# The down weights of experts 4 to 63: requested from ScalarE's queue, behind the first half of the output copy

## The chip, the core and the metric

The kernel runs on one core of a Trainium2 chip. The metric is the time of one execution on the device in microseconds (us); the median of several runs counts. The core has five engines that run side by side and wait for each other by semaphores: TensorE (PE in the profile, its weight loads PEld), VectorE (DVE), ScalarE (ACT), GpSimd (POOL) and SyncE (SP). Sixteen DMA engines move data between the device memory and the on-chip memory. They take their work from queues, which SyncE, ScalarE or GpSimd fill.

## The reference, cut to what matters

One layer of a decoder: a mixer of two recurrent branches, a normalisation, then a mixture of experts with a shared expert, a gated embedding, and a second normalisation. The change lies in the 64 routed experts:

```python
for c in range(N_EXPERTS // EXPERT_CHUNK):          # 64 experts in all
    g = jnp.einsum('td,edf->tef', xt, w_gate[sl])
    u = jnp.einsum('td,edf->tef', xt, w_up[sl])
    hdn = jax.nn.silu(g) * u * combine[:, sl, None]
    y = y + jnp.einsum('tef,efd->td', hdn, w_down[sl])
```

There are 512 tokens of 1,024 values, each sent to 8 of 64 experts. An expert has gate and up weights of 1,024 x 256 and down weights of 256 x 1,024, in 32-bit floats, 1 MB each. Tokens are gathered by expert in tiles of 96 rows.

## The kernel before

The expert stage runs from about 760 to 1,416 us of the profiled execution. Every expert takes the same steps, one expert after the other:

- GpSimd gathers the expert's rows from device memory, four experts ahead (the gather, line 663).
- SyncE requests the weights: `load_in` gate and up (two DMAs of 1 MB, line 522), `load_down` the down weights (one DMA of 1 MB, line 525). There are four buffers of each kind, so the weights of expert e + 4 go where those of expert e were. Gate and up may be requested once TensorE has done the gate and up products of expert e (semaphore `g_e_put`), the down weights once it has done the down products of expert e (`y_e_put`).
- Products are made in three passes of a faster number format: ScalarE makes the high part of the weights (`gate_up_high`, `down_high`), VectorE subtracts it to get the low part (`gate_up_low`, `down_low`), and TensorE multiplies high by high, low by high and high by low (lines 732 to 734). Line 1169 is the helper for all ScalarE operations, line 1425 that for VectorE's element-wise ones.
- TensorE works in the order: gate and up products of expert u, turning of the rows of expert u + 1 (8 transposes, line 739), down products of expert u - 1, turning of the hidden values of expert u (2 transposes).
- `y_kept` copies the result out of two banks of TensorE's memory, the first half on ScalarE (96 x 512), the second on VectorE (line 1984). GpSimd then adds the rows into `acc_dram` in device memory (`add_rows`, line 677, the scatter below). One scatter is issued only when the one before has landed, and `y_kept` of an expert waits until the scatter of two experts before has landed (`rows_added`), since there are two buffers `yb`.

The order on every engine is written out by hand. ScalarE's, in `expert`: high part of the next gate and up weights, silu, high part of the next rows, high part of this expert's down weights, `y_kept` of the expert before, high part of the hidden values. SyncE's is a loop over the experts: wait for `g_e_put`, request gate and up, wait for `y_e_put`, request down. Since TensorE makes the down products of expert u - 1 only after the gate and up products of expert u, SyncE stands at `y_e_put` of expert u - 1 when `g_e_put` of expert u is already there, and gate and up of expert u + 4 are requested behind it.

Of the kernel before, what the change touches and what calls it, by code (L numbers as in the profile page):

```python
# [42 lines left out]
E = 64  # L43
# [30 lines left out]
def decoder_layer(nc, A, out):  # L74
# [9 lines left out]
    with ctx:  # L84
# [14 lines left out]
        def sem(name):  # L99
            return ctx.enter_context(nc.semaphore(name))  # L100
# [164 lines left out]
        dn_row = [v.rearrange("p k c -> p (k c)") for v in dn]  # L265
# [79 lines left out]
        S = {n: sem(n) for n in names}  # L345
# [3 lines left out]
        s_wdn = [sem(f"expert_down{u}") for u in range(4)]  # L349
# [6 lines left out]
        def wait(eng, s, v):  # L356
            if not isinstance(v, int) or v > 0:
                eng.wait_ge(s, v)
# [17 lines left out]
        for h in range(CB // HD):  # L376
            r0 = h * HD
            while r0 < (h + 1) * HD:
                n = min((h + 1) * HD, (r0 // P + 1) * P) - r0
                PIECES.append((h, r0 - h * HD, n, r0 // P, r0 % P))  # L380
                r0 += n
        PAIRS = [(k, m) for m in range(ML) for k in range(ML)
                 if any(t == k and h * HD < (m + 1) * P and (h + 1) * HD > m * P for h, _, _, t, _ in PIECES)]
        LRU_BANKS = [2, 3, 0, 1, 2, 3]
        G_BANKS = [3, 0, 1]

        @block.sync
        def _(sp):
# [129 lines left out]
            w_down_e = A["moe_w_down"][0].rearrange("e (p k) c -> e p (k c)", k=2)  # L518

            def load_in(e, u, done):  # L520
                for w, src in enumerate((w_gate_e, w_up_e)):
                    sp.dma_start(gu_row[u][w], src[bass.ds(e, 1)].rearrange("o p x -> p (o x)")).then_inc(done, 16)

            def load_down(e, u, done):
                sp.dma_start(dn_row[u], w_down_e[bass.ds(e, 1)].rearrange("o p x -> p (o x)")).then_inc(done, 16)
# [21 lines left out]
            with sp.Fori(0, E // 4 - 1) as i:  # L547
                for u in range(4):
                    sp.wait_ge(S["g_e_put"], 4 * i + (u + 1))
                    load_in(4 * i + (4 + u), u, s_wgu[u])  # L550
                    sp.wait_ge(S["y_e_put"], 4 * i + (u + 1))
                    load_down(4 * i + (4 + u), u, s_wdn[u])

            sp.wait_ge(S["y_e_put"], E)
            sp.wait_ge(S["texp_ready"], 1)
# [1 line left out]
            with sp.If(n_over > 0):  # L557
                with sp.Fori(0, OV) as i:
                    with sp.If(i < n_over):
                        e = sp.value_load(texpi[0:1, bass.ds(i, 1)].bitcast(i32), min_val=0, max_val=E - 1)  # L560
# [606 lines left out]
        def _(act):  # L1167
            def f(out_, in_, func, **kw):
                return nc.scalar.activation(out_, in_, func, **kw)  # L1169
# [167 lines left out]
            def rows_high(i, u):  # L1337
                act.wait_ge(S["xT_e_put"], 4 * i + u + 1)
                for h in range(2):
                    f(xe_hi[:, 4 * h:4 * h + 4], banks[h][:, 0:4 * SL].rearrange("p (k x) -> p k x", k=4),  # L1340
                      ACT.Copy).then_inc(S["xT_e_high"], 1)

            def gate_up_high(i, u):
                act.wait_ge(s_wgu[u % 4], 32 * i + 32 * (u // 4 + 1))
                wait(act, S["g_e_put"], 4 * i + u - 1)
                for k in range(2):
                    for w in range(2):
                        ks = slice(KD * w + 4 * k, KD * w + 4 * k + 4)
                        f(gu_hi[u % 2][:, w, 4 * k:4 * k + 4], gu_raw[u % 4][:, ks], ACT.Copy).then_inc(S["gu_e_high"], 1)


            def down_high(i, u):
                act.wait_ge(s_wdn[u % 4], 16 * i + 16 * (u // 4 + 1))
                wait(act, S["y_e_put"], 4 * i + u - 1)
                if isinstance(i, int) and i == 0 and u == 1:
                    act.wait_ge(S["acc_stored"], 16 * TT)
                f(dn_hi[u % 2], dn[u % 4][:, 0], ACT.Copy).then_inc(S["dn_e_high"], 1)

            def hid_high(i, u):
                act.wait_ge(S["hT_e_put"], 4 * i + u + 1)  # L1360
                f(heT_hi[u % 2], banks[4][:, 0:SL], ACT.Copy).then_inc(S["hT_e_high"], 1)

            def y_kept(i, u):
                wait(act, S["rows_added"], 64 * i + 16 * (u - 1))
                act.wait_ge(S["y_e_put"], 4 * i + u + 1)
                f(yb[u % 2][:, 0:512], banks[5][0:SL, :], ACT.Copy).then_inc(S["y_e_act"], 1)

            def expert(i, u, more=True):
                if more:
                    gate_up_high(i, u + 1)  # L1370
                act.wait_ge(S["g_e_put"], 4 * i + u + 1)
                wait(act, S["hT_e_put"], 4 * i + u - 1)
                f(hid_e[u % 2], banks[2 + u % 2][0:SL, 0:F], ACT.Silu).then_inc(S["silu_e"], 1)
                if more:
                    rows_high(i, u + 1)
                down_high(i, u)
                if not isinstance(i, int) or u >= 1:
                    y_kept(i, u - 1)
                hid_high(i, u)

            def sh_silu(t):
# [12 lines left out]
            for u in range(0, 5):  # L1394
                expert(0, u)
            with act.Fori(1, E // 4 - 1) as i:
                for u in range(1, 5):
                    expert(i, u)
            for n in range(E - 3, E):
                expert(0, n, more=n + 1 < E)  # L1400
            y_kept(0, E - 1)

            act.wait_ge(S["texp_ready"], 1)
# [667 lines left out]
```

## Time and profile before

| | us |
|---|---|
| median of 3 runs | 1435.78 (1435.25 to 1435.85) |
| the profiled execution, whole | 1443.62 |
| its span, first to last instruction | 1441.9 |
| expert stage, first expert's rows high to the last scatter landed | about 779 to 1416 |
| TensorE busy in the span | 1371.3 (95%) |
| ScalarE busy | 689.6 (48%) |
| VectorE busy | 978.7 (68%) |

Times inside the execution are counted from the start of the span. The busy share of TensorE is counted from matmuls that overlap, so it doesn't say that TensorE is never late; the time between the same operation of two neighbouring experts (the period) says more. A DMA's landing is the time from its issue to the moment its semaphore is full. The profile gives it for the down weights and the scatters; for gate and up, which share one semaphore, the chain of work shows it.

### The profile page before, as it was taken

How to read it: one execution, taken by the hardware profiler on the slowest of the kernel's cores; microseconds unless marked ns; L12 is line 12 of the kernel's file. 1: busy time of each engine (PE TensorE's matmuls, PEld its weight loads, DVE VectorE, ACT ScalarE, POOL GpSimd, SP SyncE). 2: the span in 40 equal slices, each digit the busy share in tenths (PEclk: the TensorE clock that was granted, in tenths of full speed). 3: DMA queues.
4: the chain of work that ended last, by engine and by line, in shares of the span. 5: the costliest groups of instructions: out<-in, count | busy, mean ns of one | idle time of the engine just before them, and what ended most of it. 6: DMA issues, size and time to landing. Idle time of an engine off the chain costs nothing.

```text
span 1441.9 us, 19598 instructions
## 1 busy us (share of the span) xinstructions
PE 1371.3 (95%) x6615; PEld 983.6 (68%) x6615; DVE 978.7 (68%) x1419; ACT 689.6 (48%) x990; POOL 485.3 (34%) x380
## 2 busy tenths in 40 slices
PE   7979999999999999999999999999999999999990
PEld 6766777777788888885545666666666666666660
DVE  7997868786611211558626888888778788788775
ACT  4233654638422222210023776766766667667650
POOL 0231534435444444000010333334344443343422
PEclk8998999999999999999999999999999999999996
DMA  8044253534233333741057999999999999999964
GB/s 257 3 132 72 76 74 81 86 66 106 80 95 95 95 102 106 307 164 67 0 200 305 347 368 363 359 363 371 366 372 365 370 375 367 372 368 362 371 201 131
DMA packets 140775, 315.82 MB, mean 219 GB/s; under 512 B 18112, under 2 KB 99696, under 8 KB 115312
## 3 DMA queue, kind: packets, MB, share of 16 engines
q1 hardware_dynamic: 126384, 281.50, 55.8%
q0 software_dynamic: 14336, 33.59, 9.7%
q8 instruction: 35, 0.57, 0.2%
q14 instruction: 20, 0.16, 0.0%
HBM read 297.27 MB, written 34.54 MB: 230 GB/s over the span
## 4 chain that ended last, share of the span: by engine, by line
PE 67%; DVE 12%; DMA 9%; DVEq 4%; issue 3%; POOL 2%; ACT 2%; POOLq 1%; SPq 1%; ACTq 0%
PE bank L732 16%; PE bank L734 15%; PE bank L733 15%; DMA gate_up<-moe_w_up_in 8%; DVE arena L1425 6%; PE bank L1104 6%; DVEq L1422 4%; PE bank L739 4%; PE bank L891 3%; PE bank L969 2%; PE bank L989 1%; DVE arena L1713 1%; POOLq L632 1%; DVE arena L1428 1%; POOL arena L633 1%
## 5 line engine op out<-in xcount | busy, mean ns | idle before, releaser
L1425 DVE TENSOR_TENSOR gate_up_low<-gate_up,gate_up_high 128x1024 fp32r<-128x1024 f32 x256 | 296.4, 1219 | 89.4 <-ACT gate_up_high L1169 89.4
L1169 ACT ACTIVATE gate_up_high<-gate_up 128x1024 fp32r<-128x1024 f32 x256 | 249.6, 1048 | 85.5 <-DMA gate_up<-moe_w_up_in 85.5
L1169 ACT ACTIVATE arena<-bank 96x512 f32<-96x512 f32 (+5 forms) x244 | 129.1, 553 | 255.8 <-PE bank L734 132.1
L677 POOL DMA_INDIRECT acc_dram<-arena x64 | 118.5, 1851 | 333.7 <-DMA acc_dram<-arena 291.6
L1425 DVE TENSOR_TENSOR arena<-arena 128x512 f32<-128x512 f32 (+12 forms) x296 | 206.7, 730 | 16.6 <-ACT arena L1169 3.6
L732 PE MATMUL bank<-gate_up_high,rows_high 128*96 128x512 f32 x512 | 206.9, 404 | 4.1 <-DVE rows_low L1425 3.7
L734 PE MATMUL bank<-gate_up_high,rows_low 128*96 128x512 f32 x512 | 203.0, 396 | 0.0
L733 PE MATMUL bank<-gate_up_low,rows_high 128*96 128x512 f32 x512 | 201.6, 394 | 0.0
L739 PEld LDWEIGHTS bank<-arena 96*128 96x128 f32 (+5 forms) x1001 | 127.3, 186 | 53.2 <-issue 37.4
L595 POOL TENSOR_TENSOR wb_low<-arena,wb_high 128x1024 fp32r<-128x1024 f32 (+1 forms) x40 | 107.1, 2682 | 147.7 <-ACT wb_high L1169 147.7
L739 PE MATMUL bank<-arena 96*128 96x96 f32 (+5 forms) x1001 | 127.3, 266 | 7.6 <-DMA arena<-x_in 4.5
L595 POOL TENSOR_TENSOR wa_low<-arena,wa_high 128x1024 fp32r<-128x1024 f32 x24 | 62.8, 2627 | 202.3 <-ACT wa_high L1169 202.3
L1104 PE MATMUL bank<-down,arena 128*96 128x512 f32 x256 | 130.6, 592 | 0.0
L660 POOL COPY arena<-arena 96x1 int32 (+1 forms) x64 | 70.5, 1101 | 128.3 <-DVEq L1422 81.7
L1169 ACT ACTIVATE wb_high<-arena 128x1024 fp32r<-128x1024 f32 (+1 forms) x40 | 45.6, 1145 | 138.4 <-DMA arena<-w_glu_in 74.2
L732 PEld LDWEIGHTS bank<-gate_up_high,rows_high 128*96 128x96 f32 x512 | 84.0, 164 | 38.8 <-DVE rows_low L1425 5.4
L734 PEld LDWEIGHTS bank<-gate_up_high,rows_low 128*96 128x96 f32 x512 | 82.9, 162 | 36.3
L1431 DVE SCALAR_TENSOR_TENSOR arena<-bank,arena 128x511 f32<-128x511 f32 (+3 forms) x44 | 32.2, 747 | 109.6 <-PE bank L734 105.0
L733 PEld LDWEIGHTS bank<-gate_up_low,rows_high 128*96 128x96 f32 x512 | 83.3, 163 | 32.3 <-issue 0.3
L1169 ACT ACTIVATE arena<-arena 128x512 f32<-128x512 f32 (+5 forms) x54 | 31.6, 609 | 154.1 <-DVE arena L1425 80.8
L663 POOL DMA_INDIRECT arena<-x_dram,arena x64 | 76.5, 1195 | 55.8 <-DVE arena L1984 31.3
L732 PE MATMUL bank<-x_high,wa_high 128*128 128x512 f32 x192 | 77.8, 405 | 8.9 <-DVE arena L1431 7.0
(172 smaller groups left out, 2645.8 us busy)
## 6 DMA issues: line engine op xcount, KB each, us to landing
gate_up<-moe_w_gate_in SPq DMA_DIRECT2D x64, 1024.0 KB
gate_up<-moe_w_up_in SPq DMA_DIRECT2D x64, 1024.0 KB
down<-moe_w_down_in SPq DMA_DIRECT2D x64, 1024.0 KB, 16.2
arena<-w_in_in SPq DMA_DIRECT2D x40, 512.0 KB, 4.0
arena<-w_glu_in SPq DMA_DIRECT2D x16, 512.0 KB, 3.9
arena<-w_lru_out_in SPq DMA_DIRECT2D x8, 768.0 KB, 4.8
arena<-x_in SPq DMA_DIRECT2D x8, 512.0 KB, 5.1
wu<-w_in_in SPq DMA_DIRECT2D x8, 512.0 KB, 6.2
```

The costliest lines, as they stand in the source:

```text
L595: nc.gpsimd.tensor_tensor(lo, w, hi.bitcast(f32), ALU.subtract).then_inc(S["w_split"], 1)
L660: nc.gpsimd.tensor_copy(idxcol[:, u:u + 1].bitcast(i32), idxT[:, bass.ds(e, 1)].bitcast(i32)).then_inc(S["slot_col"], 1)
L663: nc.gpsimd.indirect_dma_start(out=xg[u], out_offset=None, in_=x1_dram, in_offset=bass.IndirectOffsetOnAxis(ap=idxcol[:, u:u + 1].bitcast( ...
L677: nc.gpsimd.indirect_dma_start(out=acc_dram, out_offset=bass.IndirectOffsetOnAxis(ap=idxcol[:, 4 + c:5 + c].bitcast(u32), axis=0), in_=yb[ ...
L732: mm(dst, w_hi, v_hi, start=start, stop=False)
L733: mm(dst, w_hi, v_lo, start=False, stop=False)
L734: return mm(dst, w_lo, v_hi, start=False, stop=stop)
L739: return nc.tensor.transpose(dst, src, ident[0:n, 0:n])
L1104: last = mm(banks[5 + hf][0:SL, :], heT[u % 2], dn[u % 4][:, 1, hs], start=False, stop=True)
L1169: return nc.scalar.activation(out_, in_, func, **kw)
L1422: dve.drain()
L1425: return V_.tensor_tensor(out_, a, b_, op)
```

## The change

SyncE's loop no longer requests the down weights of experts 4 to 63; it only waits for `g_e_put` and requests gate and up. ScalarE requests them in `expert`, behind `y_kept` of the expert before, and ahead of the high part of the hidden values. The wait that protects the buffer is the one that `y_kept` makes anyway (`y_e_put`). The down weights of experts 0 to 3 stay with SyncE.

```diff
                 for u in range(4):
                     sp.wait_ge(S["g_e_put"], 4 * i + (u + 1))
                     load_in(4 * i + (4 + u), u, s_wgu[u])
-                    sp.wait_ge(S["y_e_put"], 4 * i + (u + 1))
-                    load_down(4 * i + (4 + u), u, s_wdn[u])
...
-            def expert(i, u, more=True):
+            w_down_e = A["moe_w_down"][0].rearrange("e (p k) c -> e p (k c)", k=2)
+
+            def expert(i, u, more=True, more_down=True):
...
                 if not isinstance(i, int) or u >= 1:
                     y_kept(i, u - 1)
+                    if more_down:
+                        nc.scalar.dma_start(dn_row[(u - 1) % 4], w_down_e[bass.ds(4 * i + (u + 3), 1)].rearrange("o p x -> p (o x)")
+                                            ).then_inc(s_wdn[(u - 1) % 4], 16)
                 hid_high(i, u)
...
             for n in range(E - 3, E):
-                expert(0, n, more=n + 1 < E)
+                expert(0, n, more=n + 1 < E, more_down=False)
```

SyncE's queue in the loop over the experts, before (two of the four experts of a turn; `gate_up_169` and `down_173` are the first pair of buffers, `gate_up_170` and `down_174` the second; the REGISTER_ALU and ISA rows work out addresses and counts):

```order
L522 ISA [waits g_e_put]
L522 DMA gate_up_169<-moe_w_gate_in 128x2048
L522 DMA gate_up_169<-moe_w_up_in 128x2048
L525 DMA down_173<-moe_w_down_in 128x2048 [waits y_e_put]
L549 REGISTER_ALU
L522 ISA [waits g_e_put]
L522 DMA gate_up_170<-moe_w_gate_in 128x2048
L522 DMA gate_up_170<-moe_w_up_in 128x2048
L525 DMA down_174<-moe_w_down_in 128x2048 [waits y_e_put]
```

And in the changed kernel:

```order
L522 ISA [waits g_e_put]
L522 DMA gate_up_169<-moe_w_gate_in 128x2048
L522 DMA gate_up_169<-moe_w_up_in 128x2048
L549 REGISTER_ALU
L522 ISA [waits g_e_put]
L522 DMA gate_up_170<-moe_w_gate_in 128x2048
L522 DMA gate_up_170<-moe_w_up_in 128x2048
```

The request of the down weights and its wait for `y_e_put` are gone from between two pairs of gate and up.

ScalarE's queue in the same loop, before, one expert (the ACTIVATE of 96x256 is the silu, that of 96x512 is `y_kept`):

```order
L1169 ACTIVATE arena<-bank 96x256 [waits hT_e_put,g_e_put]
L1338 REGISTER_ALU
L1169 ACTIVATE rows_high<-bank 128x384 [waits xT_e_put]
L1169 ACTIVATE rows_high<-bank 128x384
L1169 ACTIVATE down_high_189<-down_175 128x1024 [waits y_e_put,expert_down2]
L1169 ACTIVATE arena<-bank 96x512 [waits y_e_put,rows_added]
L1169 ACTIVATE hidden_high_185<-bank 128x96 [waits hT_e_put]
L1344 REGISTER_ALU
L1169 ACTIVATE gate_up_high_179<-gate_up_169 128x1024 [waits g_e_put,expert_in0]
```

And in the changed kernel (its helper for ScalarE stands at line 1167):

```order
L1167 ACTIVATE arena<-bank 96x256 [waits hT_e_put,g_e_put]
L1167 ACTIVATE rows_high<-bank 128x384 [waits xT_e_put]
L1167 ACTIVATE rows_high<-bank 128x384
L1167 ACTIVATE down_high_189<-down_175 128x1024 [waits y_e_put,expert_down2]
L1167 ACTIVATE arena<-bank 96x512 [waits y_e_put,rows_added]
L1380 ISA
L1380 DMA down_174<-moe_w_down_in 128x2048
L1167 ACTIVATE hidden_high_185<-bank 128x96 [waits hT_e_put]
L1342 REGISTER_ALU
L1167 ACTIVATE gate_up_high_179<-gate_up_169 128x1024 [waits g_e_put,expert_in0]
```

The request stands behind `y_kept` without a wait of its own, with one instruction for its address ahead of it, and `hidden_high` and the next `gate_up_high` stand behind it.

## Rows read from the trace of the kernel before

**Rows 1.** The page: DMA busy share and GB/s in 40 slices.

```profile
DMA  8044253534233333741057999999999999999964
GB/s 257 3 132 72 76 74 81 86 66 106 80 95 95 95 102 106 307 164 67 0 200 305 347 368 363 359 363 371 366 372 365 370 375 367 372 368 362 371 201 131
```

**Rows 2.** Busy time by stretch: PE, PEld, DVE, ACT, POOL, clock, DMA share, GB/s.

```profile
788.00:792.00 4.00, 4.00 (x21) 2.81 (x20) 1.84 (x4) 2.20 (x4) 0.00 (x0) 1.00 0.00 0
796.00:800.00 4.00, 4.00 (x23) 3.09 (x22) 3.65 (x4) 2.26 (x5) 3.11 (x4) 1.00 0.97 358
960.00:980.00 20.00, 20.00 (x91) 13.57 (x91) 16.66 (x22) 12.78 (x20) 7.83 (x8) 1.00 1.02 355
1100.00:1120.00 20.00, 19.76 (x90) 13.37 (x89) 16.03 (x22) 13.58 (x21) 8.64 (x8) 1.00 1.02 373
```

**Rows 3.** The DMA queues in the 100 us from 1060, ten experts.

```profile
q1 hardware_dynamic: 4361, 31.76, 81.1%
q0 software_dynamic: 2240, 5.19, 21.3%
```

**Rows 4.** The chain that ended last: start us, us, what.

```profile
779.00 0.87 PE bank L739 x8
...
1032.44 0.86 PE bank L739 x8
...
1336.01 22.26 DMA gate_up<-moe_w_up_in
...
1371.19 0.86 PE bank L739 x8
...
1380.93 0.86 PE bank L739 x8
...
1390.67 0.86 PE bank L739 x8
```

**Rows 5.** SyncE's queue in order of time: start us, us, request; the first experts.

```profile
792.91 0.33 SPq L525 DMA_DIRECT2D down<-moe_w_down_in  x1
793.51 0.76 SPq L522 DMA_DIRECT2D gate_up<-moe_w_gate_in  x1
...
802.65 0.33 SPq L525 DMA_DIRECT2D down<-moe_w_down_in  x1
```

**Rows 6.** ScalarE in order of time: silu of experts 1 and 2; idle in brackets.

```profile
788.95 0.38 ACT L1169 ACTIVATE arena<-bank 96x256 f32<-96x256 f32 x1 [3.32 <-PE bank L734]
...
798.69 0.38 ACT L1169 ACTIVATE arena<-bank 96x256 f32<-96x256 f32 x1 [1.26 <-PE bank L734]
```

**Rows 7.** ScalarE around the place of the new request, a late expert.

```profile
1106.73 0.59 ACT L1169 ACTIVATE arena<-bank 96x512 f32<-96x512 f32 x1 [0.89 <-PE bank L1104]
...
1109.71 3.90 ACT L1169 ACTIVATE gate_up_high<-gate_up 128x1024 fp32r<-128x1024 f32 x4 [2.25 <-DMA gate_up<-moe_w_up_in]
```

**Rows 8.** An early expert, VectorE's last row part and TensorE's product behind it.

```profile
858.50 1.02 DVE L1425 TENSOR_TENSOR rows_low<-bank,rows_high 128x384 fp32r<-128x384 f32 x2 [0.37 <-ACT rows_high L1169]
...
861.03 0.45 PE L732 MATMUL bank<-gate_up_high,rows_high 128*96 128x512 f32 x1
```

**Rows 9.** Landing of the down weights: 790 to 880 us, then 1,100 to 1,390 us.

```profile
DMA to landing us min/median/max: 7.1/7.8/8.6
...
DMA to landing us min/median/max: 15.2/16.2/17.0
```

**Rows 10.** Landing of the scatters: 1,100 to 1,388 us, then 1,388 to 1,442 us.

```profile
DMA to landing us min/median/max: 6.4/9.0/9.8
...
DMA to landing us min/median/max: 4.4/4.6/5.1
```

**Rows 11.** GpSimd, two scatters in a row; and the next output copy on ScalarE.

```profile
1104.90 2.13 POOL L677 DMA_INDIRECT acc_dram<-arena  x1 [4.92 <-DMA acc_dram<-arena]
...
1114.79 1.96 POOL L677 DMA_INDIRECT acc_dram<-arena  x1 [4.63 <-DMA acc_dram<-arena]
...
1116.95 0.59 ACT L1169 ACTIVATE arena<-bank 96x512 f32<-96x512 f32 x1 [1.35 <-PE bank L1104]
```

## Prediction

> **What bounds the kernel now.** I read the slices of the page first: from the 24th on the DMA row says 9 and about 365 GB/s without a break [rows 1]. The busy time by stretch sharpens this: the DMA engines stand at 1.02 both at 960 us, where TensorE has no gap, and at 1,100 us, where it is short of 20 us by 0.24 [rows 2]. So in the expert stage the DMA engines are full, and the question is how close behind them TensorE is.
>
> The chain answers that. The 8 transposes of line 739 come once per expert. The first time stands at 779.00, the last at 1390.67, and there are 62 periods between: 611.67 / 62 = 9.87 us. Where TensorE never waits, the period is 1380.93 - 1371.19 = 9.74 us. From 1032.44 to 1390.67 there are 36 periods, 358.23 us, and 36 x 9.74 is 350.6: the starving of TensorE costs 7.6 us in all. The chain gives its cause: it runs through landings of `up` weights in the late part, the last for 22.26 us from 1336.01 to 1358.3. Behind that landing the period is 9.74 again (1371.19, 1380.93, 1390.67) [rows 4]. So **the end of the kernel hangs on the moment at which that late pair of gate and up weights has landed**; it moves as this landing moves, and the most that can be won is 7.6 us.
>
> How much DMA work is an expert? In 100 us with ten experts the queue of the weights took 81.1% of the engines and that of gathers and scatters 21.3% [rows 3]: 8.1 us and 2.1 us per expert, together 102%, since packets overlap a little. A third of 8.1, **2.7 us, is the price of 1 MB of weights**.
>
> **Part 1: gate and up are requested earlier.** SyncE stands at `y_e_put` while `g_e_put` is there. For the sixth expert: the pair is requested at 793.51, behind the down request of 792.91 [rows 5], though the silu that waits for the same `g_e_put` starts at 788.95 [rows 6]. The change requests it about 0.1 us after, at 789.1, 4.4 us earlier. This holds for 59 experts, but in a full queue an earlier request only waits longer. It counts where the DMA engines are idle, and that is in one place: 788 to 792 us, share 0.00, and full again by 796 us [rows 2]. There the engines start 4.4 us earlier. They then have 3 loads (the pair, and the down weights, which come at 793.6), 8.1 us, and are through at about 797.3; the next pair may be requested at 798.8, behind the silu of 798.69 [rows 6], where today the work lasts until 793.5 + 8.1 = 801.6 and the next request comes at 802.65 with scatter and gather between. So a new hole of 1.5 us opens, and 4.4 - 1.5 = **2.9 us** of DMA time are won. Bounds: 1.9 (the loads run a tenth faster than in the crowd, and the hole is 2.5) and 4.4 (no hole, scatter and gather fill it).
>
> **Part 2: the down weights go through another queue.** In one queue, requests are served in their order: the down weights of expert e stand behind gate and up of e, and land 16.2 us after the request in the late part, 7.8 us in the early part [rows 9]. In the changed kernel the request is ScalarE's, its queue holds nothing else, and SyncE's queue is full. Take the pair requested today right behind the down request that follows the `y_kept` of 1106.73, at about 1107.6; with the 22.3 us of the chain's landing [rows 4] it lands at 1129.9. In the changed kernel its down weights are requested about one period after 1107.3, the end of `y_kept` [rows 7], at 1117.2, that is 12.7 us ahead of the landing of the pair. If two queues share the engines, a load of 2.7 us takes 5.4 us, and 2.1 us more for gather and scatter: it lands at about 1125, ahead of the pair that is needed first. So one more load is served before each late `up` weight: **+2.7 us** on the landing that sets the end. Bounds: 0 (the engines serve by time of request) and 4.0 (half of the following down load gets ahead as well).
>
> That the engines mix queues shows in the scatters: one lands after 9.0 us while the weights' queue is full and after 4.6 us when it is empty [rows 10]; it is slowed, but it doesn't wait for the 16 to 22 us of requests ahead of it. The Trainium skill ("DMA: Bandwidth & Descriptors", section "Queues, rings and completion order") says that each DMA engine takes packets in turn from the queues that have work. By that rule part 2 costs 2.7 us; by service in time order it would cost nothing, and no run so far shows two such queues of weights.
>
> **Part 3: the request itself on ScalarE.** A request took 0.33 us on SyncE, and from one to the next, with the address, 0.60 us (792.91 to 793.51) [rows 5]. The trace has none on ScalarE; I take 0.6 us, once per expert, with 0.3 and 1.2 (twice the value) as bounds. What is queued behind: `hidden_high`, and the next `gate_up_high`. In the late part `gate_up_high` first waits 2.25 us for the DMA [rows 7], which hides 0.6 and 1.2 alike. In the early part there is no such wait, and the cover is further down: VectorE's last part of the rows ends at 858.50 + 1.02 = 859.52 and TensorE starts the product at 861.03 [rows 8], 1.5 us later. So part 3 costs 0. If the cover were gone it would cost up to 0.6 us per expert. SyncE loses a request and a wait, which nobody waits for. The down weights of the last experts have over 10 us to spare in both orders.
>
> **The sum**, against the profiled execution: -2.9 + 2.7 + 0 = -0.2 us on a span of 1441.9 us; the execution of 1443.6 us stays at 1443.4. The runs that count lie at 1435.8, so 1435.6. Bounds: -4.4 + 0 = -4.4 and -1.9 + 4.0 = +2.1, thus **1431.4 to 1437.9** for this case.
>
> **Rival A: the scatters become the bound (slower).** They are a chain of their own: 1104.90, next 1114.79, that is 9.89 us, and GpSimd waits for the landing of the one before [rows 11]. The period of the experts is 9.95 us there. The landing at 1114.8 is 2.2 us ahead of the `y_kept` at 1116.95 that needs it. One full queue beside them lengthens a scatter from 4.6 to 9.0 us, by 4.4 us [rows 10]. ScalarE's queue is a second one, and has work for 5.4 of every 9.95 us, beginning right where a scatter is under way. If it slows the scatter in the same measure, that is 4.4 x 5.4 / 9.95 = 2.4 us; it decides from 0.1 us on, since the chain has no more room, and after 2.2 / 2.4, about one expert, `y_kept` waits on ScalarE with everything behind it. Against it: as soon as the period is longer than the 10.2 us that the DMA work of an expert takes by [rows 3], the engines have pauses and the crowding goes. So the period settles between 9.95 and 10.2. At 10.1 from the start: 62 x (10.1 - 9.87) = +14 us, **1450**; at 10.2 it is +20, and with 0.1 us of slowing it is +3. The early part speaks against it too: there the scatters keep up with a period of 9.74 us, so they have a little room. The rule of turns that the Trainium skill's page on DMA states makes this rival likelier, since a third queue with work takes a turn of its own; that can't be seen in the trace of before.
>
> **Rival B: the earlier requests count in full (faster).** If down weights don't get ahead, or two queues keep the engines a little fuller than one, the landings come 2.9 to 4.4 us earlier, and at most the 7.6 us of starving go: 1428.2 to 1432.9, taken as **1431**. For it: TensorE has nothing else to wait for. Against it: the share is 1.02 already.
>
> **Rival C: ScalarE's request is dear (slower).** If it held ScalarE for 3 us, more than the 2.25 and the 1.5 us of cover, 0.8 to 1.5 us per expert would show, 60 x 1 = +60 us. SyncE's 0.33 us speak against it. And that the change does nothing, because its requests come no earlier, is excluded by the 4.4 us between [rows 5] and [rows 6]; what is left of that case is the forecast.
>
> **How the numbers follow.** Forecast 0.45, rival A 0.34, B 0.17, C 0.04. About 0.2% (2.9 us) can be told from no change. The forecast's own range reaches below that bound a little: faster 0.17 + 0.04 = 0.21; of rival A a part (slowing of some tenths) stays below it: slower 0.31 + 0.04 = 0.35; same 0.44. The range that should hold 8 in 10 goes from 1430 to 1452: below it lies half of B, above it C and the dear end of A.
>
> **What would show it.** Part 1: in the stretch 788 to 792 us the DMA share is no longer 0, and the pair's request stands at 789. Part 2: the down weights land in about 8 us in the late part instead of 16; the landings of `up` take some 4 us longer counted from their request. Part 3: `gate_up_high` still waits for the DMA in the late part. Rival A: landings of scatters over 9.5 us, a `y_kept` on ScalarE that waits for `acc_dram`, and pauses in the DMA share. The forecast is wrong if the period in the late part leaves 9.95 by more than 0.1 us.

## The result, and the profile after

The changed kernel takes 1445.65 us, median of 4 runs (1443.33 to 1446.72), against 1435.82 for the kernel before beside it (1435.25 to 1439.39). The ratio is 1.0061, with a 95% interval of 1.0045 to 1.0077: it is slower, by 9.8 us. Timed again with the last experiments (e11_after_again) it gave 1445.5 us and 1.006 [1.0041, 1.0078].

The two profiled executions hide this. The changed kernel's took 1443.33 us with a span of 1441.6 us, that of before 1443.62 and 1441.9. The reason lies ahead of the change's place. VectorE's first and last output copy frame the expert stage; start, duration, engine and operation, before and then after:

```profile
792.92 0.69 DVE L1984 COPY arena<-bank 96x512 f32<-96x512 f32 x1
...
1408.49 0.69 DVE L1984 COPY arena<-bank 96x512 f32<-96x512 f32 x1 [3.63 <-PE bank L1104]
```

```profile
783.81 0.69 DVE L1987 COPY arena<-bank 96x512 f32<-96x512 f32 x1
...
1408.05 0.69 DVE L1987 COPY arena<-bank 96x512 f32<-96x512 f32 x1 [3.63 <-PE bank L1102]
```

The stage itself, from its first to its last output copy, went from 615.6 to 624.2 us, **+8.7 us**, while in the execution of before everything ahead of it took 9.1 us longer (in 100 to 200 us its granted clock was 0.95, and 1.00 in the other). From here on this stage time is what is compared. It comes from one execution of each kernel; the changed kernel's, taken twice, differs by 1.2 us (624.2 and 625.4).

The wait that grew is in the groups of the page. Of the changed kernel, two of ScalarE and one of GpSimd (busy, mean ns, then idle time and its releaser):

```profile
L1167 ACT ACTIVATE arena<-bank 96x512 f32<-96x512 f32 (+5 forms) x244 | 129.3, 553 | 337.6 <-DMA acc_dram<-arena 155.2
L1167 ACT ACTIVATE gate_up_high<-gate_up 128x1024 fp32r<-128x1024 f32 x256 | 249.4, 1049 | 2.7 <-issue 2.3
...
L675 POOL DMA_INDIRECT acc_dram<-arena x64 | 99.3, 1552 | 320.7 <-DMA acc_dram<-arena 286.7
```

ScalarE's output copies (96x512) now wait 155.2 us for the landing of scatters, and `gate_up_high` no longer waits for weights at all; in [rows 7] it was the other way round. The chain that ended last says the same: its share of DMA was 9%, mostly `up` weights [rows 4 show one of them], and now it is

```profile
PE 39%; DMA 36%; DVE 11%; issue 5%; DVEq 4%; POOL 2%; POOLq 2%; ACT 1%; SPq 0%; ACTq 0%
```

nearly all of the 36% landings of scatters into `acc_dram`. Here is the same place as in [rows 7], a late expert on ScalarE, in order of time:

```profile
1107.32 0.60 ACT L1167 ACTIVATE arena<-bank 96x512 f32<-96x512 f32 x1 [2.74 <-DMA acc_dram<-arena]
1107.47 0.34 ACTq L1380 DMA_DIRECT2D down<-moe_w_down_in  x1
1107.86 0.25 ACT L1167 ACTIVATE hidden_high<-bank 128x96 fp32r<-128x96 f32 x1
1108.01 3.89 ACT L1167 ACTIVATE gate_up_high<-gate_up 128x1024 fp32r<-128x1024 f32 x4
```

The copy waited 2.74 us for a scatter; the request took 0.34 us of ScalarE's queue; what stands behind it waits for nothing.

**Where in the stage the time went.** In blocks of ten experts, from one output copy on ScalarE to the tenth after it:

| experts | 1-10 | 11-20 | 21-30 | 31-40 | 41-50 | 51-60 |
|---|---|---|---|---|---|---|
| before | 97.4 | 97.4 | 99.0 | 100.0 | 98.1 | 100.2 |
| changed | 97.4 | **106.1** | 99.3 | 100.9 | 98.7 | 98.4 |

The whole loss is in one block; the four blocks behind it sum to 397.3 us in both kernels. What happens in the long block is seen in ScalarE's output copies, 9.73 us apart up to 890.98 and then 10.7, 11.6 and 11.0:

```profile
881.25 0.59 ACT L1167 ACTIVATE arena<-bank 96x512 f32<-96x512 f32 x1 [1.35 <-PE bank L1102]
890.98 0.59 ACT L1167 ACTIVATE arena<-bank 96x512 f32<-96x512 f32 x1 [1.35 <-PE bank L1102]
901.70 0.59 ACT L1167 ACTIVATE arena<-bank 96x512 f32<-96x512 f32 x1 [2.33 <-DMA acc_dram<-arena]
913.26 0.59 ACT L1167 ACTIVATE arena<-bank 96x512 f32<-96x512 f32 x1 [4.16 <-DMA acc_dram<-arena]
924.27 0.59 ACT L1167 ACTIVATE arena<-bank 96x512 f32<-96x512 f32 x1 [4.45 <-DMA acc_dram<-arena]
```

and in the chain of work of the same stretch (start, us, what), which holds nothing but scatters and GpSimd's 0.9 us between them:

```profile
868.23 10.02 DMA acc_dram<-arena
...
879.15 10.82 DMA acc_dram<-arena
...
890.87 10.80 DMA acc_dram<-arena
...
902.58 10.66 DMA acc_dram<-arena
...
947.47 9.29 DMA acc_dram<-arena
```

10.8 + 0.9 is 11.7 us per scatter in this stretch; from the second expert to the twelfth it is 10.7 on average, while an expert takes 9.73. So the scatter falls behind its output copy, from 1.9 us at the second expert to 11.6 us at the twelfth. There the two buffers `yb` are used up, and the output copy, hence TensorE, goes at the pace of the scatters.

The DMA share has no pauses in this (busy time by stretch, columns as in [rows 2]):

```profile
920.00:960.00 40.00, 36.97 (x159) 24.16 (x159) 29.25 (x42) 22.95 (x35) 15.78 (x15) 1.00 1.02 367
1100.00:1120.00 20.00, 18.82 (x84) 12.42 (x83) 17.99 (x24) 14.82 (x23) 10.38 (x11) 1.00 1.02 351
```

TensorE is busy for 37 of 40 us at 920 to 960, and the DMA engines for all of them. So they moved weights that nobody waited for yet. That lead comes back nowhere: the changed kernel's engines run dry earlier at the end. Before, and then after:

```profile
1370.00:1380.00 10.00, 10.00 (x47) 6.82 (x46) 8.31 (x12) 7.02 (x11) 2.50 (x2) 1.00 1.02 361
1380.00:1400.00 20.00, 20.00 (x91) 13.57 (x90) 14.85 (x21) 10.92 (x18) 6.04 (x6) 1.00 0.58 178
```

```profile
1370.00:1380.00 10.00, 10.00 (x47) 6.82 (x46) 8.83 (x13) 7.50 (x11) 3.63 (x4) 1.00 0.79 261
1380.00:1400.00 20.00, 20.00 (x92) 13.59 (x91) 13.92 (x20) 9.71 (x18) 6.64 (x6) 1.00 0.36 51
```

With the stage ending at 1408 in both, before has 10 x 1.02 + 20 x 0.58 = 21.8 us of DMA work left from 1370 on, after has 10 x 0.79 + 20 x 0.36 = 15.1: the changed kernel has fetched weights worth 6.7 us sooner than needed. That this lead was piled up in the long block alone isn't shown: the smaller hole at the start of the stage (below, part 1) also gave the engines a few us.

### The profile page after: what moved, and what is told of

It is laid out like the page before. It is cut to its first block, busy times and chain, and to the rows that moved or that the text cites. A ratio compares the mean times of both kernels' runs of the same rounds, so it can differ in the third digit from the quotient of the medians.

```text
span 1441.6 us, 19610 instructions
## 1 busy us (share of the span) xinstructions
PE 1370.1 (95%) x6615; PEld 979.8 (68%) x6615; DVE 978.7 (68%) x1419; ACT 690.4 (48%) x990; POOL 505.6 (35%) x380
## 4 chain that ended last, share of the span: by engine, by line
PE 39%; DMA 36%; DVE 11%; issue 5%; DVEq 4%; POOL 2%; POOLq 2%; ACT 1%; SPq 0%; ACTq 0%
DMA acc_dram<-arena 35%; PE bank L730 9%; PE bank L732 9%; PE bank L731 8%; DVE arena L1428 6%; DVEq L1425 4%; PE bank L889 3%; PE bank L967 2%; PE bank L987 1%; DVE arena L1716 1%; POOLq L630 1%; POOL arena L631 1%; PE bank L1061 1%; DVE arena L1431 1%; PE bank L737 1%
## 5 line engine op out<-in xcount | busy, mean ns | idle before, releaser
L1167 ACT ACTIVATE arena<-bank 96x512 f32<-96x512 f32 (+5 forms) x244 | 129.3, 553 | 337.6 <-DMA acc_dram<-arena 155.2
L1428 DVE TENSOR_TENSOR arena<-arena 128x512 f32<-128x512 f32 (+12 forms) x296 | 204.3, 722 | 16.2 <-ACT arena L1167 3.2
L675 POOL DMA_INDIRECT acc_dram<-arena x64 | 99.3, 1552 | 320.7 <-DMA acc_dram<-arena 286.7
L737 PE MATMUL bank<-arena 96*128 96x96 f32 (+5 forms) x1001 | 128.5, 267 | 10.7 <-DMA arena<-x_in 4.8
L658 POOL COPY arena<-arena 96x1 int32 (+1 forms) x64 | 85.5, 1336 | 128.3 <-DVEq L1425 81.7
L661 POOL DMA_INDIRECT arena<-x_dram,arena x64 | 70.1, 1095 | 55.8 <-POOL arena L658 53.9
L1987 DVE COPY arena<-bank 96x512 f32<-96x512 f32 x64 | 43.9, 687 | 61.0 <-DMA acc_dram<-arena 55.5
```

What stands on the lines that cost most here:

```text
L658: nc.gpsimd.tensor_copy(idxcol[:, u:u + 1].bitcast(i32), idxT[:, bass.ds(e, 1)].bitcast(i32)).then_inc(S["slot_col"], 1)
L661: nc.gpsimd.indirect_dma_start(out=xg[u], out_offset=None, in_=x1_dram, in_offset=bass.IndirectOffsetOnAxis(ap=idxcol[:, u:u + 1].bitcast( ...
L675: nc.gpsimd.indirect_dma_start(out=acc_dram, out_offset=bass.IndirectOffsetOnAxis(ap=idxcol[:, 4 + c:5 + c].bitcast(u32), axis=0), in_=yb[ ...
L737: return nc.tensor.transpose(dst, src, ident[0:n, 0:n])
L1428: return V_.tensor_tensor(out_, a, b_, op)
```

## The experiments

The theory to be tested: the second queue slows the scatters while SyncE's queue is full; they are a chain, which loses about 1 us per expert until the buffers are used up; from then on the output copies wait. Rival 1: the time is lost on the weights (down weights get ahead of late `up` weights). Rival 2: gate and up came too early. Rival 3: ScalarE's request is dear. All stage times and blocks are from one profiled execution of each kernel, the ratios from timed runs against the kernel before, which was timed again beside each group: 1438.0 us beside e1, e2 and e5, 1436.6 beside e3, e4, e6 and e7, 1437.8 beside e8 to e11. So medians of different groups are compared by their ratios.

| kernel | median us | ratio [95%] | stage | blocks of ten |
|---|---|---|---|---|
| before | 1435.8 | | 615.6 | 97.4 97.4 99.0 100.0 98.1 100.2 |
| changed | 1445.7 | 1.0061 [1.0045, 1.0077] | 624.2 | 97.4 106.1 99.3 100.9 98.7 98.4 |
| e1_one_queue | 1429.5 | 0.9938 [0.9919, 0.9957] | 609.9 | 97.4 97.4 97.4 97.4 97.6 98.9 |
| e5_late_in | 1468.4 | 1.0228 [1.0204, 1.0253] | 648.6 | 101.6 107.3 106.1 104.3 104.5 100.4 |
| e3_two_sums_after | 1436.7 | 0.9996 [0.9982, 1.001] | 617.1 | 97.4 97.7 99.8 99.4 99.6 99.6 |
| e4_two_sums_before | 1437.0 | 1.0002 [0.9987, 1.0017] | 617.3 | 97.4 99.6 100.0 99.1 98.4 99.3 |
| e2_eighth | 1697.4 | 1.176 [1.1717, 1.1803] | | |
| e6_eighth_cols | 1436.9 | 1.0000 [0.9985, 1.0015] | 618.7 | 97.4 97.4 97.4 100.6 101.2 101.3 |
| e7_half_cols | 1439.3 | 1.0016 [0.9997, 1.0035] | 617.5 | 97.4 97.4 99.8 101.0 99.4 101.0 |
| e8_late_half | 1442.3 | 1.0035 [1.002, 1.005] | 622.0 | 97.4 97.4 97.4 103.1 103.7 99.6 |
| e9_early_half | 1437.7 | 1.0002 [0.9984, 1.002] | 618.5 | 102.5 101.6 99.0 97.3 97.4 97.4 |
| e10_later_place | 1446.3 | 1.0065 [1.0044, 1.0086] | 625.0 | 101.9 102.9 99.3 99.0 99.2 99.2 |
| e11_after_again | 1445.5 | 1.006 [1.0041, 1.0078] | 625.4 | 97.4 106.6 99.0 99.6 99.7 99.6 |

### The early request alone: e1_one_queue

SyncE keeps all requests, but asks for the next pair of gate and up as soon as `g_e_put` is there, and for the down weights after it:

```diff
+            sp.wait_ge(S["g_e_put"], 1)
+            load_in(4, 0, s_wgu[0])
...
                 for u in range(4):
-                    sp.wait_ge(S["g_e_put"], 4 * i + (u + 1))
-                    load_in(4 * i + (4 + u), u, s_wgu[u])
+                    sp.wait_ge(S["g_e_put"], 4 * i + (u + 2))
+                    load_in(4 * i + (5 + u), (u + 1) % 4, s_wgu[(u + 1) % 4])
                     sp.wait_ge(S["y_e_put"], 4 * i + (u + 1))
                     load_down(4 * i + (4 + u), u, s_wdn[u])
```

> Gate and up are requested as early as in the changed kernel, but the down weights stay in SyncE's queue, so there is no second queue of weights (SyncE asks for the pair of expert n + 5 first, then waits for y_e_put and asks for the down weights of expert n + 4). Theory A (the second queue of weights lengthens the chain of scatters, which takes the lead of the early experts): no slowing, 0 to -4 us against the kernel before, ScalarE's output copy not waiting for acc_dram. Theory B (ScalarE's 60 requests cost the 9 us): the same, 0 to -4 us. Theory C (the earlier requests of gate and up crowd the scatters): +6 to +10 us, as the changed kernel.

It is **faster than both kernels**: 1429.5 us, 8.5 us less than the kernel before beside it, where 0 to 4 were expected. The stage is 5.7 us shorter. That would be the 2.9 us of part 1 and about 2.7 us, one load, since a pair now stands one down load further ahead in the queue; no run separates the two. Waits of the stage (what waited, for what: us in total, times, longest):

```profile
ACT arena L1177 <- PE bank L1112: 84.8, 62, 4.1
...
ACT gate_up_high L1177 <- DMA gate_up<-moe_w_up_in: 36.9, 25, 2.7
```

against the changed kernel's

```profile
ACT arena L1167 <- DMA acc_dram<-arena: 155.2, 50, 4.6
```

The pair of e1_one_queue is requested as early as that of the changed kernel, so rival 2 falls: the loss belongs to the second queue.

### The second queue alone: e5_late_in

The changed kernel, but SyncE waits for `y_e_put` before it requests gate and up, as late as before:

```diff
-                    sp.wait_ge(S["g_e_put"], 4 * i + (u + 1))
+                    sp.wait_ge(S["y_e_put"], 4 * i + u)
                     load_in(4 * i + (4 + u), u, s_wgu[u])
```

> As the changed kernel, with the down weights on ScalarE's queue, but gate and up requested as late as before (at y_e_put of the expert before). Theory A: slower by 5 to 12 us than the kernel before, output copies wait for acc_dram, lag of the scatters behind the output copy grows from 2 to about 11 us in the first 15 experts. Theory B: +6 to +10 us too, but without waits for acc_dram. Theory C (early gate and up are the cause): within 2 us of the kernel before.

Much slower, 1468.4 us, 30 us above the kernel before where 5 to 12 were expected, and the stage is 33 us longer. The copies wait for scatters 52 times, 193.1 us. A `y_e_put` that is late because of a scatter here also delays the next pair, and from the eleventh expert to the fiftieth the pace stays at 10.4 to 10.7 us. The early requests are thus worth 24 us of stage beside a second queue, not 3. That they do it by keeping the delay from feeding back into the loads is my reading of the order of the requests.

### Without the chain of scatters: e3_two_sums_after, e4_two_sums_before

Scatters of odd experts go to a second sum in device memory, so a scatter waits only for the one two before it. The second sum is not read, so the output lacks the odd experts. The same edit in the changed kernel and in that of before:

```diff
-                wait(pool, S["rows_added"], 16 * n)
+                    wait(pool, RA[k[1] % 2], 32 * k[0] + 16 * (k[1] // 2))
...
-                    out=acc_dram, out_offset=...
+                    out=(acc_dram, acc2_dram)[0 if k is None else k[1] % 2], out_offset=...
```

> The changed kernel with its scatters taken out of their chain: experts of even and odd number are added into two sums in device memory, each scatter waits only for the one two before (as the two output buffers need anyway), and both sums are first stored from the same rows (4 more stores of 512 KB ahead of the stage). The odd experts' sum isn't read at the end, so half of the experts is missing from the output. Theory A (the chain of scatters, slowed by the second queue, holds the experts): its loss goes away; within 4 us of e4_two_sums_before or faster than it by up to 8 us, as e1 was than the kernel before. Theory B (ScalarE's requests cost) or a theory of less DMA throughput with two queues: it stays 7 to 16 us slower than e4 or than e4 less 8 us.

> The kernel before with the same two sums (the odd experts' sum isn't read at the end). The chain of scatters wasn't what TensorE waited for there, so all theories expect only the price of the 4 added stores: 0 to +6 us against the kernel before.

The changed kernel's loss is gone: 1436.7 and 1437.0 us, stages of 617.1 and 617.3. No copy waits for `acc_dram`, and the waits for weights are back (changed kernel with two sums, the stage):

```profile
ACT gate_up_high L1174 <- DMA gate_up<-moe_w_up_in: 75.6, 44, 3.2
```

This pair is the case that the forecast described, a kernel whose end hangs on the weights alone: early requests and a second queue cancel there, as the sum of -0.2 said, though intervals of some 2 us to either side would hide a small effect. It rules out rivals 1 and 3, whose costs would stand in e3_two_sums_after too.

The pair shows one thing more. The scatters are slowed by the second queue here too, where each waits only for the one two before it. Landings at 1,060 to 1,160 us, kernel before and then changed kernel, both with two sums:

```profile
gate_up<-moe_w_up_in SPq DMA_DIRECT2D x10, 1024.0 KB, 21.2
acc_dram<-arena POOLq DMA_INDIRECT x10, 8.6
```

```profile
gate_up<-moe_w_up_in SPq DMA_DIRECT2D x10, 1024.0 KB, 25.8
...
acc_dram<-arena POOLq DMA_INDIRECT x10, 9.6
```

### How much second queue it takes: e2_eighth, e6_eighth_cols, e7_half_cols

All three are e1_one_queue with part of each down load moved to ScalarE's queue, at the place of the change: 16 of 128 partitions, 256 of 2,048 columns, 1,024 of 2,048 columns. For the last:

```diff
+            def load_down_rest(e, u, done):
+                sp.dma_start(dn_row[u][:, 1024:2048], ...[:, 1024:2048]).then_inc(done, 16)
...
+                        nc.scalar.dma_start(dn_row[(u - 1) % 4][:, 0:1024], ...[:, 0:1024]
```

> As e1, but ScalarE requests 16 of the 128 partitions of each of the 60 down loads at the place of the changed kernel, SyncE the other 112: as many requests on ScalarE, with an eighth of the bytes. Theory A (bytes of a second queue slow the scatters): within 2 us of e1. Theory B (the request itself on ScalarE is what costs): +6 to +10 us against the kernel before. Theory C: as e1.

> As e1, but ScalarE requests the first 256 of 2,048 columns of each down load on all 128 partitions (an eighth of the bytes, rows of 1 KB) and SyncE the other 1,792. Theory A: little in the second queue, so within 0 to 5 us of e1. Theory B (60 requests on ScalarE): 8 to 16 us slower than e1. If e2 was slow for its 16 and 112 partitions and not for its second queue, this one doesn't show e2's 244 GB/s but 350 to 370.

> As e6, with half of the columns (1,024, rows of 4 KB) from ScalarE's queue. Theory A: between e6 and the changed kernel, that is 4 to 12 us slower than e1. Theory B: as e6.

e2_eighth is a miss, 1697.4 us where it was to stay within 2 us of e1_one_queue. It says nothing on queues, because with the load split by partitions the DMA engines are slow altogether (its 1,060 to 1,160 us):

```profile
DMA packets 4432, 24.38 MB, mean 244 GB/s; under 512 B 1036, under 2 KB 1036, under 8 KB 1878
...
down<-moe_w_down_in SPq DMA_DIRECT2D x7, 896.0 KB, 9.7
down<-moe_w_down_in ACTq DMA_DIRECT2D x7, 128.0 KB, 46.1
```

The two pieces of a load share a semaphore, so the view can't tell which of them landed first: it shows only that a first piece had landed after 9.7 us and a second after 46.1.

The split by columns keeps 363 and 366 GB/s, but it isn't free either: in e6_eighth_cols the queues of weights take 76.7 + 4.3 = 81.0% of the engines for 29.63 + 1.33 = 30.96 MB, 2.62% per MB, against 80.2% for 31.30 MB, 2.56%, in e1_one_queue. That is 2% of 8.1 us, 0.2 us per expert, and the weights are late from the 30th expert on (69.9 us of waits for `up`). Its copies wait for scatters for only 4.0 us. By the ratios it is 9 us slower than e1_one_queue, where 0 to 5 were expected, and rival 3 had said 8 to 16; but e3_two_sums_after makes the same 60 requests on ScalarE and loses nothing by them, and the waits here are for weights. With half of the load in e7_half_cols the waits for scatters are 90.9 us in 34 copies, with all of it 155.2 in 50. So the waits grow with the share of the second queue; the times of these two don't tell what they cost, since the split costs something too.

### The second queue for half of the experts: e8_late_half, e9_early_half; and at another place: e10_later_place

Experts 4 to 35 by one queue and 36 to 63 by two, and the reverse; and the changed kernel with the request behind the next `gate_up_high`. These three and e11_after_again were timed together.

```diff
+            for lo, hi, own in ((0, 8, True), (8, E // 4 - 2, False)):
...
+                        if own:
+                            sp.wait_ge(S["y_e_put"], 4 * i + (u + 1))
+                            load_down(4 * i + (4 + u), u, s_wdn[u])
```

> SyncE requests the down weights of experts 4 to 35 as in e1_one_queue, ScalarE those of experts 36 to 63 as in the changed kernel; gate and up early throughout. Theory 'the scatter chain has a lead, the second queue eats it, and then the experts run at the pace of the chain': the lead of the chain in e1_one_queue is some 8 us when ScalarE takes over; ten experts later it is gone, and then the blocks of ten experts cost about 100 us or more: stage 2 to 8 us longer than in e1_one_queue, loss after expert 42. Rival 'only the start of the stage is delicate': a second queue from the middle on costs under 1 us.

> ScalarE requests the down weights of experts 4 to 35, SyncE those of experts 36 to 63. Theory 'lost lead': the same loss as in the changed kernel in experts 11 to 20 (block of about 106 us), stage 6 to 12 us longer than in e1_one_queue; once one queue holds all weights again, the lag of the scatter falls from about 12 us and no output copy waits for acc_dram. Rival 'only the start is delicate': the same loss too, so that e8 and e9 together tell: by the theory both lose, by the rival only this one.

> The changed kernel, but ScalarE's request of the down weights stands behind the next high part of gate and up, some 4.5 us later, well inside the flight of the scatter instead of at its start. If what costs is a second full queue of weights beside the scatters, whatever its phase: stage within 3 us of the changed kernel's, output copies still wait for acc_dram. If what costs is that the request meets the scatter's start: the loss of 8 us mostly goes, lag of the scatter behind the output copy below 5 us.

> The changed kernel once more, beside the other three on one chip. Every theory: 8 to 11 us slower than the kernel before (ratio 1.0055 to 1.0075), stage from the first to the last output copy some 624 us, with the block of experts 11 to 20 the long one. If the long block stands elsewhere or is missing, the loss hangs on chance in the order of packets and not on the lag reached by then.

e11_after_again repeats the changed kernel, long block and all. e10_later_place loses the same; its scatters are 12.1 us behind already at the seventh expert. The loss falls early in e9_early_half too, where experts 1 to 10 take 102.5 us and not, as expected, 11 to 20 about 106. Yet up to 835 us its weights are requested at the same times as the changed kernel's, to 0.2 us; only, its third scatter took 14.3 us to land. So what decides where the loss begins is open. Its size is steady: experts 1 to 30 take 302.8 us in the changed kernel, 303.0 in e11_after_again, 303.1 in e9_early_half and 304.1 in e10_later_place, against 292.2 in e1_one_queue. e8_late_half and e9_early_half both lose, so the start of the stage isn't special, as the theory said. The loss in e8_late_half is larger than I expected, 12.1 us against e1_one_queue instead of 2 to 8, and it has two parts. The first is not the scatters:

```profile
1115.76 0.59 ACT L1180 ACTIVATE arena<-bank 96x512 f32<-96x512 f32 x1 [1.35 <-PE bank L1115]
1115.91 0.34 ACTq L1393 DMA_DIRECT2D down<-moe_w_down_in  x1
...
1122.76 3.90 ACT L1180 ACTIVATE gate_up_high<-gate_up 128x1024 fp32r<-128x1024 f32 x4 [6.21 <-DMA gate_up<-moe_w_up_in]
```

Right after the change of queues `gate_up_high` waits 6.21 us and then 3.98 us for `up` weights, one of which needs 31.06 us to land: `up` weights landed some 23 us after their request in this stretch, so SyncE's queue was that far behind, and the down loads in ScalarE's queue get ahead of a pair that is needed first. Two periods of 12.75 and 12.43 us instead of 9.74 cost 5.7 us. This is part 2 of the prediction, twice its size, seen bare. Then the scatters fall behind within four experts, and experts 41 to 50 take 103.7 us.

**Why the scatter slows at first and less later.** Landings in the same three stretches of 40 us (800, 840 and 880 us on), first with all weights in one queue (e8_late_half), then with two (e11_after_again):

```profile
acc_dram<-arena POOLq DMA_INDIRECT x4, 8.9
...
acc_dram<-arena POOLq DMA_INDIRECT x4, 8.9
...
acc_dram<-arena POOLq DMA_INDIRECT x4, 8.9
```

```profile
acc_dram<-arena POOLq DMA_INDIRECT x4, 9.5
...
acc_dram<-arena POOLq DMA_INDIRECT x3, 10.0
...
acc_dram<-arena POOLq DMA_INDIRECT x4, 10.6
```

The chain takes landing + 0.9 us, so its break-even with 9.73 us is a landing of 8.8 us. With one queue it stands right on it; with two it is 0.7 to 1.8 us beyond. Behind the long block the landing is down to 9.1 (1,060 to 1,160 us of the same run):

```profile
q1 hardware_dynamic: 2876, 20.94, 55.1%
q10 hardware_dynamic: 1440, 10.49, 25.5%
q0 software_dynamic: 2270, 5.24, 21.8%
...
gate_up<-moe_w_up_in SPq DMA_DIRECT2D x10, 1024.0 KB, 11.7
down<-moe_w_down_in ACTq DMA_DIRECT2D x10, 1024.0 KB, 9.5
acc_dram<-arena POOLq DMA_INDIRECT x11, 9.1
```

`up` weights need 11.7 us there, and needed 17.9 us at 880 to 920. The delay of the output copies has worked off SyncE's queue by 6.2 us. My reading is that the three queues then have work together less often, and scatters are quick enough for a period of 9.93 us (397.3 / 40), the one that the kernel before has in the same experts, where weights are its bound. So the loss would stop by itself after some 8 us, as the price of working off that queue. That fits the 6.7 us of unused lead at the end, and e9_early_half, where the rest of the stage runs on one queue at 9.73 us and rebuilds the queue (`up` needs 16.0 us again at 1,260 us): its stage is 6.9 us shorter than e11_after_again's, and 8.6 longer than that of e1_one_queue. Its scatters never catch up, though: they stay 9 to 10 us behind, with landings of 8.8 us. e3_two_sums_after speaks for it as well: there SyncE's queue stays long (25.8 us for `up` at 1,060 to 1,160 us) and the scatters still need 9.6 us beside the second queue. But that the shorter queue and not something else that changed with it quickens the scatter is inferred from these landings; no run held one and varied the other.

## Why the prediction was wrong, by its own steps

- **Part 1 held.** The pair is requested at 779.98, 3.8 us ahead of the first output copy, where it was 0.6 us behind it [rows 5]: 4.4 us earlier, as said. The hole in the DMA share [rows 2] shrinks. The ten us around the first output copy, before and then after (the latter 9 us earlier, like the copy):

```profile
786.00:796.00 10.00, 10.00 (x47) 6.83 (x46) 7.04 (x11) 5.28 (x9) 1.40 (x3) 1.00 0.23 79
```

```profile
777.00:787.00 10.00, 10.00 (x47) 6.80 (x46) 8.57 (x12) 6.47 (x11) 1.51 (x3) 1.00 0.85 302
```

That is 6.2 us of DMA time more; in e11_after_again the share is 0.70, 4.7 us more, and in e1_one_queue 0.62, 3.9 us more. So the 2.9 us were too small, in the changed kernel even the upper bound of 4.4. What this DMA time is worth in the stage can't be read from the changed kernel; e1_one_queue's -5.7 us leaves room for it.

- **Part 2 held as a mechanism.** Down weights passed the queued pairs: in the late part they landed after 9.5 us (e11_after_again) where 8 was forecast and 16.2 had been [rows 9]. Against part 1 the sum was -0.2, and e3_two_sums_after against e4_two_sums_before measured -0.2 us of stage and -0.3 us of time. That two terms cancel so exactly says little, as the intervals are ten times wider and part 1 won more DMA time than forecast. In the changed kernel itself the sign expected of `up` (4 us longer) didn't show: there the waits for scatters had shortened the queue. Where they are out of the way it does, with 25.8 us in e3_two_sums_after against 21.2 in e4_two_sums_before.
- **Part 3 held**: 0.34 us for the request, nothing behind it waits. The cover that was named, a wait of `gate_up_high` for weights in the late part, is gone; it is hidden by the output copy's own wait for the scatter.
- **The failed step is the weighing of rival A, and in it the sentence that in the early part the scatters "keep up with a period of 9.74 us, so they have a little room"**. They had none. In the trace of before, scatters landed like this in the stretches of 40 us from 800, 840 and 880 us:

```profile
acc_dram<-arena POOLq DMA_INDIRECT x4, 9.5
...
acc_dram<-arena POOLq DMA_INDIRECT x4, 9.0
...
acc_dram<-arena POOLq DMA_INDIRECT x4, 8.8
```

With GpSimd's 0.9 us behind each that is 10.4, 9.9 and 9.7 us, where an expert took 9.74. The trace shows the lag too: from the sixth expert on the scatters are some 6 us behind the output copies, more than half of what two buffers allow, and up to the 22nd they never gain on them. [rows 11] was read for the late part alone, where the longer period hides it. The forecast took the weights as the sole bound, where the chain of scatters was a second one on the same footing. So its sum had no term for the scatters; the term measures 8.9 us of stage, from +8.7 with the chain to -0.2 without it (e3_two_sums_after against e4_two_sums_before). A kernel with two bounds that close doesn't keep a sum made against one of them.

- **Rival A's marks**: landings over 9.5 us were seen (10.0 to 10.8 in the long block, 9.1 later), output copies waiting for `acc_dram` too. Pauses in the DMA share were not: the engines stay at 1.02. So its settling was thought out wrongly. It had the period rise a little, to 10.1, for all 62 experts, because the engines would pause; in fact it rises to about 11 for five experts, the engines go on and pile up a lead, and then the period is what it was. It gave +14 and +9.8 was measured: right side, right wait, wrong course, so that the number came near is partly luck.
- **Rival B** did not happen in the changed kernel. That the early requests can pay is seen without the second queue (e1_one_queue, 1429.5 us), there with one load more of lead. **Rival C** fell with part 3.

The Trainium skill bears on this in one place. The row first: with the down weights in ScalarE's queue a scatter on GpSimd's queue took 10.6 us to land instead of 8.9 (880 to 920 us of e11_after_again and of e8_late_half), at total rates of 364 and 361 GB/s. "DMA: Bandwidth & Descriptors", section "Issuing engines are not separate DMA queues", says that starting transfers from several engines only saves the sequencer's time, as all run on the same engines. For the rate the runs agree. The section doesn't say who gets it, and that is where the time went here.

## What to carry to other kernels

With DMA engines that are full, as here, a second queue of weights raised no rate. It lengthened the landings in the other queues (e3_two_sums_after against e4_two_sums_before), and what paid was the chain whose next transfer waits for the landing of the last. Before such a change, put landing plus issue of that chain beside the period: if they are within some tenths of a us, the chain is a second bound, whatever its engine's idle time says. What was good in this change, the early request of the pair, could be had inside one queue by changing the order of two requests (e1_one_queue).

## What the hardware showed that was not expected

- A 1 MB load of 128 partitions split into 112 and 16 partitions on two queues brought the rate down to 244 GB/s (1,060 to 1,160 us, share of the engines 1.02 as ever), and the later piece landed after 46.1 us. The split by columns into the same sizes kept 363 GB/s. The cause is open.
- Down loads that passed some 23 us of queued requests (e8_late_half) made `up` weights land after 31.06 us, and TensorE lost 5.7 us in two experts. That the price of a second queue depends on how full the first is at that moment is an inference from this one place.
- The part ahead of the expert stage varied by 9.1 us between two profiled executions, as much as the change's effect; spans alone would have said that nothing had changed.
